# Neighbourhood attention on one Trainium2 core: transposing the probabilities by a product with diag(1/sum), and a quarter of the evictions on VectorE

## The chip, the cores and the metric

One core of one Trainium2 chip runs the whole program; all data is fp32. The metric is the device time of one execution in microseconds. Of the core's engines three do the work of the stage at hand: TensorE (matrix products and transposes into PSUM), VectorE and ScalarE (everything elementwise, and the moves out of PSUM, called evictions here).

## The reference, cut to what matters

The model is a block with four mixers and experts, followed by two layers of a second block. Each of these two layers has a neighbourhood attention: 512 tokens stand on a grid of 8 rows by 64 columns, with 8 heads of width 64. A query attends in one softmax to its window of the grid (all 8 rows, 16 columns, with a bias per offset) and to 256 context keys.

```
s_win = einsum("bhqd,ibhqjd->bhqij", q_r, k_win) * scale + bias
s_ctx = einsum("bhqd,bkhd->bhqk", q_r, k_ctx) * scale
p = softmax(concatenate([s_win, s_ctx], axis=-1), axis=-1)
o = einsum("bhqij,ibhqjd->bhqd", p_win, v_win) + einsum("bhqk,bkhd->bhqd", p_ctx, v_ctx)
```

## The kernel before, in words

A tile of 128 queries takes, in the order in which the kernel holds the tokens, the keys of its own 128 tokens and of 64 on either side. `neighbourhood_attention` (line 3143) runs once per layer. It makes queries, keys and values first, and then builds a list of *quads*: one quad is a pair of heads and two query tiles, so a layer has 4 pairs x 2 = 8 quads. A quad has two *steps*, one per query tile t (0 to 3), each with two *entries*, one per head. A layer has 16 steps; four of them in a row make a pair of heads. An entry has n local keys (192 for t of 0 and 3, 256 for t of 1 and 2) and 256 context keys, so its row of scores is 448 or 512 wide.

`attend` (line 411) turns the quads into groups. For step i:

- *score* (lines 427 to 435, TensorE): q against the keys, with 64 contraction rows, into two PSUM banks, one per head. Its eviction is the *mask* (line 440, VectorE): it adds the bias table (or zeros) and writes S in SBUF, with partial maxima, and line 444 reduces them.
- *exp* (line 454, ScalarE): in place in S, with the sum of the row.
- *norm* (lines 469 to 476, VectorE): the reciprocal of the sums, and one `tensor_scalar` per entry that multiplies the whole row of S by it, in place.
- *turn* (lines 478 to 507): per entry one group of up to four transposes of 128 keys (or 64) into one bank, by line 492, or by a product with the identity (line 490) where the output starts at partition 64. That is the case only for t = 3, whose last local chunk has 64 keys at p0 = 64. For t = 0 the first chunk has 64 keys at p0 = 0. ScalarE evicts the bank to PT with one instruction per run of chunks that lie side by side: three for t = 0 and 3, one for t = 1, two for t = 2.
- *weigh* (lines 509 to 524, TensorE, then VectorE's copy): PT against the values, once per quad.

An fp32 product of the source appears in the trace as two records of LDWEIGHTS and MATMUL, a transpose as one. For a transpose, and for the product with the identity, the chunk of S is the loaded operand and the identity the moving one, 128 columns wide.

The order of the work is written out in lines 526 to 546. Iteration i puts score(i+2), norm(i+1), turn(i), exp(i+2), and where a quad has just ended, the weigh of the quad before. `products` (line 237) gives this list to every engine, and each engine runs its own members of it strictly in that order, with semaphores to the others: a group's products wait for what it `needs` and for the eviction of the group that had its bank; an eviction waits for its `after`. S has three slots, so the mask of step i+2 waits for the evictions of step i-1. Scores have two pairs of banks, everything else four single banks. Lines 3256 to 3259 put two remaining value products (vs) between the first iterations. `attend` also serves four other attentions, with the same code.

Of the kernel before, what the change touches and what calls it, by code (L numbers as in the profile page):

```python
# [16 lines left out]
ALU = mybir.AluOpType  # L17
# [3 lines left out]
P = 128  # L21
BANK = 512
# [195 lines left out]
def group(pe, evac, on, tile=None, after=(), needs=(), other=None, pool="", reads=(), dma=False):  # L218
    return Group(pe, evac, on, tile, after, needs, other, pool, reads, dma)
# [188 lines left out]
    return groups  # L408


def attend(M, st, name, quads, heads, nk, chunks, bufs=None, pool="scores"):

    slots = 3
    S, PT = bufs or (st.sb(f"{name}_S", [P, slots, heads, nk]), st.sb(f"{name}_PT", [P, 2, 2, chunks, 2 * P]))
    part_max = st.sb(f"{name}_part_max", [P, 4, heads, 2])
    neg_max = st.sb(f"{name}_neg_max", [P, 4, heads])
    total = st.sb(f"{name}_total", [P, 4, heads])  # L420
    scale = st.sb(f"{name}_scale", [P, 4, heads])
    steps = [(q, x, entries) for q, quad in enumerate(quads) for x, entries in enumerate(quad.steps)]
    N = len(steps)
    masked = steps[0][2][0].masks is not None
    scored, maxed, exped, normed, turned, weighed = {}, {}, {}, {}, {}, {}

    def score(i):
        entries = steps[i][2]

        def pe(pe_, bank):  # L430
            for j in range(len(entries[0].parts)):
                for e, entry in enumerate(entries):
                    c0, q, k, n = entry.parts[j]
                    last = pe_.matmul(bank[:, e * BANK + c0:e * BANK + c0 + n], q, k, start=True, stop=True)
            return last

        def mask(dve, bank, link):
            for e, entry in enumerate(entries):
                for j, (c0, n, m) in enumerate(entry.masks):
                    link.post(dve.tensor_tensor_reduce(  # L440
                        S[:, i % slots, e, c0:c0 + n], bank[:, e * BANK + c0:e * BANK + c0 + n], m, 1.0, -3.0e38,
                        ALU.add, ALU.max, part_max[:, i % 4, e, j:j + 1]))
            dve.wait_ge(link.sem, link.n)
            return dve.tensor_reduce(neg_max[:, i % 4, :], part_max[:, i % 4, :, 0:len(entries[0].masks)], AX,
                                     ALU.max, negate=True)

        def exp_bank(act, bank, link):
            return act.activation(S[:, i % slots, 0, 0:entries[0].n], bank[:, 0:entries[0].n], ACT.Exp,
                                  bias=neg_max[:, i % 4, :], accum_out=total[:, i % 4, :])

        def exp_rows(act, _, link):
            for e, entry in enumerate(entries):
                s = S[:, i % slots, e, 0:entry.n]
                last = act.activation(s, s, ACT.Exp, bias=neg_max[:, i % 4, e:e + 1],
                                      accum_out=total[:, i % 4, e:e + 1])
            return last

        free = turned.get(i - slots, [])
        if masked:
            scored[i] = group(pe, mask, "v", after=free, pool=pool)  # L460
            exped[i] = group(None, exp_rows, "s", after=(scored[i],))
        else:
            scored[i] = exped[i] = group(pe, exp_bank, "s", after=free, pool=pool)
            maxed[i] = group(None, lambda dve, _, link: dve.tensor_reduce(
                neg_max[:, i % 4, :], scored[i].bank[:, 0:entries[0].n], AX, ALU.max, negate=True),
                "v", reads=(scored[i],))
            scored[i].after += (maxed[i],)

    def norm(i):
        def ev(dve, _, link):  # L470
            link(dve.reciprocal(scale[:, i % 4, :], total[:, i % 4, :]))
            for e, entry in enumerate(steps[i][2]):
                s = S[:, i % slots, e, 0:entry.n]
                last = dve.tensor_scalar(s, s, scale[:, i % 4, e:e + 1], None, ALU.mult)
            return last
        normed[i] = group(None, ev, "v", after=(exped[i],))

    def turn(i):
        q, x, entries = steps[i]
        turned[i] = []  # L480
        free = (weighed[q - 2],) if q >= 2 else ()
        for e, entry in enumerate(entries):
            for a in range(0, len(entry.turns), 4):
                some = entry.turns[a:a + 4]

                def pe(pe_, bank, e=e, some=some):
                    for y, (c0, n, p0, _) in enumerate(some):
                        out, keys = bank[p0:p0 + n, y * P:(y + 1) * P], S[:, i % slots, e, c0:c0 + n]
                        if p0:
                            last = pe_.matmul(out, keys, M.ident[:, :], start=True, stop=True)  # L490
                        else:
                            last = pe_.transpose(out, keys, M.ident[:, :])
                    return last

                def ev(eng, bank, link, entry=entry, some=some):
                    y = 0
                    while y < len(some):
                        _, n, p0, chunk = some[y]
                        z = y + 1
                        while z < len(some) and some[z][1:] == (n, p0, chunk + z - y):  # L500
                            z += 1
                        half = entry.half * P
                        last = move(eng, PT[p0:p0 + n, q % 2, entry.head % 2, chunk:chunk + z - y, half:half + P],
                                    bank[p0:p0 + n, y * P:z * P].rearrange("p (c n) -> p c n", n=P))
                        y = z
                    return last
                turned[i].append(group(pe, ev, "s", needs=(normed[i],), after=free))

    def weigh(q):
        quad = quads[q]  # L510
        done = [g for i in range(N) if steps[i][0] == q for g in turned[i]]

        def pe(pe_, bank):
            first, count = set(), {}
            for side, *_ in quad.weigh:
                count[side] = count.get(side, 0) + 1
            for side, v, chunk, p0, n, a, b in quad.weigh:
                count[side] -= 1
                last = pe_.matmul(bank[side * HD:(side + 1) * HD, a:b], v,
                                  PT[p0:p0 + n, q % 2, side, chunk, a:b],  # L520
                                  start=side not in first, stop=count[side] == 0)
                first.add(side)
            return last
        weighed[q] = group(pe, lambda eng, bank, link: quad.out(eng, bank[:, 0:quad.width], link), "v", needs=done)

    order = []
    for i in range(-2, N + 1):
        now = []
        if i + 2 < N:
            score(i + 2)  # L530
            now.append(scored[i + 2])
            if not masked:
                now.append(maxed[i + 2])
        if 0 <= i + 1 < N:
            norm(i + 1)
            now.append(normed[i + 1])
        if 0 <= i < N:
            turn(i)
            now += turned[i]
        if i + 2 < N and masked:  # L540
            now.append(exped[i + 2])
        if i >= 1 and (i == N or steps[i][0] != steps[i - 1][0]):
            weigh(steps[i - 1][0])
            now.append(weighed[steps[i - 1][0]])
        order.append(now)
    return order
# [367 lines left out]
def branches_ab(M, oT_a, oT_b, big, c_in, c_extra):  # L914
# [4 lines left out]
    with Stage(nc, "ab") as st:  # L919
# [62 lines left out]
        with Stage(nc, "b_att") as sb:  # L982
            products(M, "b_att", sum(attend(M, sb, "b", quads, 2, T, TT), []), pools=PAIRED_BANKS)
# [2159 lines left out]
def neighbourhood_attention(M, L, l, hT, yT, sums):  # L3143
# [3 lines left out]
    with Stage(nc, f"na{l}") as st:  # L3147
        qT = st.sb("qT", [P, 4, T])
        kT = st.sb("kT", [P, 4, TA * P])
        v = st.sb("v", [P, TA, NA_W])  # L3150
# [3 lines left out]
        heads = st.sb("heads", [P, 2 * 2 * 5 * 2 * P])  # L3154
        S_rows = st.sb("S", [P, 3, 2, BANK])
# [6 lines left out]
        PT = heads[:, :].rearrange("p (q h c n) -> p q h c n", q=2, h=2, c=5)  # L3162
# [48 lines left out]
        turned = []  # L3211
        for i, (x, xT) in enumerate(((q, qT), (k, kT))):
            turned += transposes(
                M, lambda t, j, x=x: x[:, t, j * P:(j + 1) * P], None, TT, 4,
                evac=lambda eng, bank, link, j, a, n, xT=xT, i=i: scaled(
                    eng, xT[:, j, a * P:(a + n) * P], bank, gains[:, i:i + 1]),
                needs=[(g, gain) for g in made[i, 0] + made[i, 1]])
        gs = context + [gain] + qk[0] + qk[1] + bias[0:1] + qk[2] + bias[1:2] + qk[3] + bias[2:4] + qk[5] + work[0, 0]
        gs += qk[4] + work[1, 0] + qk[6] + work[1, 1] + vs[0:1] + work[0, 1] + vs[1:2] + turned
        quads = []  # L3220
        for pair in range(MH // 2):
            for t0 in range(0, TT, 2):
# [29 lines left out]
                def out(eng, bank, link, pair=pair, t0=t0):  # L3252
                    return move(eng, yT[:, pair, t0 * P:(t0 + 2) * P], bank)
                quads.append(Quad(steps, weigh, out, 2 * P))
        order = attend(M, st, f"na{l}", quads, 2, BANK, 5, (S_rows, PT))
        order[0][0].needs += tuple(context + turned)
        order[0][0].after += tuple(bias)
        order[4][-1].needs += tuple(vs)
# [932 lines left out]
```

How the kernel before makes its waits and increments, by code:

```python
    def __call__(self, ins):  # L137
        self.n += 1
        ins.then_inc(self.sem, 1)
        self.eng.wait_ge(self.sem, self.n)
# [53 lines left out]
    def load(self, sp):  # L194
        while self.issued < len(self.tiles):
            i = self.issued
            if self.slot[i] >= len(self.bufs):
                break
            if self.prior[i] is not None:
                if self.prior[i] not in self.last_group:
                    break
                sp.wait_ge(self.groups_done, self.last_group[self.prior[i]])
            src = self.tiles[i][0]
            sp.dma_start(self.view(i), src(sp) if callable(src) else src).then_inc(self.landed[self.slot[i]], 16)
            self.issued += 1
# [1 line left out]
    def arrived(self, pe, i):  # L207
        pe.wait_ge(self.landed[self.slot[i]], 16 * self.turn[i])
# [58 lines left out]
    def wait_moves(eng, of):  # L267
        for on in "vsg":
            counts = [g.count for g in of if g.on == on and not g.dma]
            if counts:
                eng.wait_ge(moved[on], max(counts))
        for g in of:
            if g.dma:
                eng.wait_ge(g.landed, 16)
# [10 lines left out]
        @block.tensor  # L285
# [5 lines left out]
                    seen = g.tile  # L291
                if g.other is not None:
                    W.arrived(pe, g.other)
                wait_moves(pe, g.needs)
                if g.before:
                    pe.wait_ge(moved[g.before.on], g.before.count)
                g.pe(pe, g.bank).then_inc(W.groups_done, 1)
# [325 lines left out]
    def first_pe(pe, bank):  # L623
        pe.wait_ge(sig["ident"], 1)
        pe.wait_ge(sig["x_in"], 16)
```

## Time and profile before

| | us |
|---|---|
| median of 3 runs (lowest, highest) | 4005.0 (4003.53, 4009.11) |
| the profiled execution, its own time | 4002.32 |
| its span, first to last instruction | 4000.6 |
| TensorE busy | 3719.4 (93%) |
| VectorE busy | 1670.9 (42%) |
| ScalarE busy | 757.1 (19%) |
| GpSimd busy | 175.2 (4%) |
| mean granted clock of TensorE | 0.970 |

Busy times are sums over the whole span, in which many stages follow each other. The time of one stage has to be read from its own window. Neighbourhood attention from its first scores to its last eviction lies from 2322 to 2396 us (layer 0) and from 3313 to 3387 us (layer 1). Ends of matrix products are modelled, so their starts are the firmer numbers. Where the trace says that an engine waited, it names the instruction that came last before it could go on.

### The profile page before, as it was taken

Reading aid. Unit: us, or ns where it says so; the run is one execution under the profiler, and the core shown is the slowest. Engines: PE = TensorE matmul, PEld = TensorE weight load, DVE = VectorE, ACT = ScalarE, POOL = GpSimd, SP = SyncE. Lnnn points to the kernel's source line nnn. Section 1 sums busy time; section 2 is a strip of 40 time slices with the busy share of each in tenths; the row PEclk is TensorE's granted clock in tenths of the full one; section 3 lists DMA queues with packets and bytes.
Section 4 is the critical chain, followed back from the end, with each engine's and each line's share of the span. In section 5 each row is a group of like instructions: output and inputs, shape, how many; then the busy total and the mean of one; then the engine's idle time right before and its main releaser. Section 6 shows DMA issues by size and latency. Waiting matters only on the chain. (4 is left out here: it accounts for less than half of the span.)

```text
span 4000.6 us, 40393 instructions
## 1 busy us (share of the span) xinstructions
PE 3719.4 (93%) x15836; PEld 2158.8 (54%) x15836; DVE 1670.9 (42%) x3004; ACT 757.1 (19%) x1707; POOL 175.2 (4%) x393
## 2 busy tenths in 40 slices
PE   8988899989799899999788999999998999999999
PEld 4654786745334345455345554488444545448844
DVE  0128533546222111111345564554455556355445
ACT  1212201211122010000224352110002435110000
POOL 1001000000000000000203000000000300000000
PEclk9989999998898999999899999999999999999999
DMA  8542012233675888988531022222223111121221
GB/s 316 179 167 96 26 54 96 85 147 121 242 288 201 321 353 334 370 335 357 193 117 62 22 70 93 76 85 85 84 84 114 43 39 47 74 89 69 85 97 51
DMA packets 197969, 576.40 MB, mean 144 GB/s; under 512 B 24580, under 2 KB 34612, under 8 KB 184776
## 3 DMA queue, kind: packets, MB, share of 16 engines
q1 hardware_dynamic: 177008, 515.15, 34.4%
q10 hardware_dynamic: 12888, 32.14, 2.3%
q0 software_dynamic: 7888, 26.53, 1.9%
q8 instruction: 129, 2.11, 0.2%
q14 instruction: 56, 0.46, 0.0%
HBM read 541.80 MB, written 32.00 MB: 143 GB/s over the span
## 5 line engine op out<-in xcount | busy, mean ns | idle before, releaser
L346 PE MATMUL ps<-out_sums 128*128 128x256 f32 (+1 forms) x1152 | 333.6, 450 | 2.3 <-issue 2.3
L346 PEld LDWEIGHTS ps<-out_sums 128*128 128x128 f32 x1152 | 218.7, 190 | 114.2 <-issue 94.5
L346 PE MATMUL ps<-ring,mixers_xT 128*128 128x256 f32 (+2 forms) x1024 | 254.0, 402 | 14.0 <-DMA ring<-in_w_in 7.1
L346 PEld LDWEIGHTS ps<-ring,mixers_xT 128*128 128x128 f32 x1024 | 195.7, 201 | 61.4 <-issue 22.2
L346 PE MATMUL ps<-mixers_xT,ring 128*128 128x512 f32 (+1 forms) x480 | 209.2, 594 | 2.6 <-DMA ring<-in_w_in 1.7
L346 PE MATMUL ps<-ring,layers_hT 128*128 128x512 f32 x416 | 187.0, 607 | 19.8 <-PEq L276 18.9
L346 PE MATMUL ps<-ring,ctx_hT 128*128 128x512 f32 (+2 forms) x448 | 166.7, 531 | 27.5 <-PEq L127 16.7
L2306 PE MATMUL ps<-ring,mixers_xT 128*64 128x512 f32 x400 | 177.1, 599 | 7.5 <-issue 6.5
L2307 PE MATMUL ps<-ring,mixers_xT 128*64 128x512 f32 x400 | 176.9, 599 | 0.0
L346 PE MATMUL ps<-ring,out_hidden 128*128 128x512 f32 x384 | 167.4, 592 | 0.0
L346 PEld LDWEIGHTS ps<-mixers_xT,ring 128*128 128x128 f32 (+1 forms) x480 | 88.6, 187 | 117.5 <-issue 113.6
L346 PEld LDWEIGHTS ps<-ring,layers_hT 128*128 128x128 f32 x416 | 79.8, 195 | 120.4 <-issue 118.1
L346 PEld LDWEIGHTS ps<-ring,ctx_hT 128*128 128x128 f32 x448 | 82.3, 196 | 107.5 <-issue 105.5
L346 PE MATMUL ps<-out_hidden 128*128 128x512 f32 x288 | 127.4, 599 | 6.2 <-issue 6.2
L2347 DVE TENSOR_TENSOR moe_h<-moe_sg,ps 128x512 f32<-128x512 f32 x17 | 11.7, 689 | 271.5 <-PE ps L2307 259.2
L2306 PE MATMUL ps<-ring,moe_hT 128*64 128x512 f32 x224 | 104.0, 619 | 21.4 <-DMA ring<-in_e_down 11.3
L346 PEld LDWEIGHTS ps<-ring,out_hidden 128*128 128x128 f32 x384 | 73.0, 190 | 91.0 <-issue 90.9
L346 PE MATMUL ps<-layers_hT,ring 128*128 128x256 f32 x512 | 115.3, 387 | 5.1 <-ACT out_rms_rs L2641 5.1
L2306 PEld LDWEIGHTS ps<-ring,mixers_xT 128*64 128x64 f32 x400 | 54.0, 138 | 121.9 <-issue 121.9
L346 PE MATMUL ps<-ring,layers_yT 128*128 128x512 f32 x256 | 112.8, 592 | 0.0
L346 PEld LDWEIGHTS ps<-layers_hT,ring 128*128 128x128 f32 x512 | 99.5, 195 | 19.6 <-issue 5.5
L346 PE MATMUL ps<-ring,ctx_ins 128*128 128x512 f32 x232 | 102.9, 602 | 6.9 <-ACT ctx_ins L3282 3.3
(855 smaller groups left out, 6057.0 us busy)
## 6 DMA issues: line engine op xcount, KB each, us to landing
ring<-in_w_ff SPq DMA_DIRECT2D x45, 2048.0 KB, 13.0
ring<-in_w_in SPq DMA_DIRECT2D x43, 2048.0 KB, 10.6
ring<-in_e_down SPq DMA_DIRECT2D x28, 2048.0 KB, 8.8
ring<-in_e_gate SPq DMA_DIRECT2D x26, 2048.0 KB, 15.9
ring<-in_e_up SPq DMA_DIRECT2D x26, 2048.0 KB, 12.6
ring<-in_w_ada SPq DMA_DIRECT2D x24, 2048.0 KB, 11.6
deep_ring_more<-in_e_up SPq DMA_DIRECT2D x7, 2048.0 KB, 9.9
deep_ring_more<-in_e_gate SPq DMA_DIRECT2D x7, 2048.0 KB, 15.5
```

The lines of the kernel that those rows point to most:

```text
L346: last = pe.matmul(out, lhsT, rhs, start=(j == 0), stop=(j == len(pairs) - 1))
L2306: pe.matmul(bank[0:HALF, :], left(k)[:, 0:HALF], wa[:, k, cols], **ends)
L2307: last = pe.matmul(bank[HALF:P, :], left(k)[:, HALF:P], wb[:, k, cols], **ends)
L2347: lambda eng, bank, link, i=i: eng.tensor_tensor(h[:, i, :], sg[:, i, :], bank, ALU.mult),
```

## The change

`attend` gets an argument `diagonal`, which only the neighbourhood attention sets. With it, norm no longer touches S: it multiplies the identity (128 x 128) by the reciprocal sums of an entry and writes a diagonal matrix `diag`, in three slots. Every transpose of a chunk of S becomes a product of that chunk with the diagonal matrix, which transposes and scales in one. And of the two evictions in steps with an odd number, the second (e = 1) is given to VectorE instead of ScalarE: 1 of 4 groups. The other attentions keep their code.

```diff
-def attend(M, st, name, quads, heads, nk, chunks, bufs=None, pool="scores"):
+def attend(M, st, name, quads, heads, nk, chunks, bufs=None, pool="scores", diagonal=False):
...
+    diag = st.sb(f"{name}_diag", [P, slots, heads, P]) if diagonal else None
...
                 s = S[:, i % slots, e, 0:entry.n]
-                last = dve.tensor_scalar(s, s, scale[:, i % 4, e:e + 1], None, ALU.mult)
+                out, s = (diag[:, i % slots, e, :], M.ident[:, :]) if diagonal else (s, s)
+                last = dve.tensor_scalar(out, s, scale[:, i % 4, e:e + 1], None, ALU.mult)
...
-                        if p0:
+                        if diagonal:
+                            last = pe_.matmul(out, keys, diag[:, i % slots, e, :], start=True, stop=True)
+                        elif p0:
                             last = pe_.matmul(out, keys, M.ident[:, :], start=True, stop=True)
                         else:
                             last = pe_.transpose(out, keys, M.ident[:, :])
...
-                turned[i].append(group(pe, ev, "s", needs=(normed[i],), after=free))
+                turned[i].append(group(pe, ev, "v" if diagonal and i % 2 and e else "s", needs=(normed[i],), after=free))
...
-        order = attend(M, st, f"na{l}", quads, 2, BANK, 5, (S_rows, PT))
+        order = attend(M, st, f"na{l}", quads, 2, BANK, 5, (S_rows, PT), diagonal=True)
```

## Rows read from the trace of the kernel before

**Rows 1.** Windows of the two attention stretches: us, busy and (instructions) of each engine, clock.
```profile
2322.00:2396.00 74.00, 66.83 (x459) 40.65 (x457) 44.15 (x203) 45.82 (x139) 0.00 (x0) 1.00 0.09 30
3312.90:3386.80 73.90, 67.67 (x459) 41.14 (x460) 44.71 (x202) 45.09 (x138) 0.00 (x0) 1.00 0.09 30
```

**Rows 2.** Timeline of TensorE: start, us, instruction, count, [idle before <-releaser].
```profile
2344.53 1.09 PE L492 MATMUL ps<-ident,na_S 128*128 128x128 f32 x8 [0.75 <-DVE na_S L474]
...
2355.36 0.38 PE L434 MATMUL ps<-na_kT,na_qT 64*128 64x256 f32 x2
2355.67 1.09 PE L492 MATMUL ps<-ident,na_S 128*128 128x128 f32 x8
2356.70 1.03 PE L434 MATMUL ps<-na_kT,na_qT 64*128 64x192 f32 x8
2358.47 1.09 PE L492 MATMUL ps<-ident,na_S 128*128 128x128 f32 x8 [0.75 <-DVE na_S L474]
```

**Rows 3.** Lines by form, layer 1's stretch: xcount | busy us, mean ns | idle before.
```profile
L492 PE MATMUL ps<-ident,na_S 128*128 128x128 f32 x112 | 17.7, 283 | 4.1 <-DVE na_S L474 4.1
L492 PE MATMUL ps<-ident,na_S 128*64 128x128 f32 x8 | 2.3, 285 | 0.0
L490 PE MATMUL ps<-ident,na_S 128*64 128x128 f32 x16 | 3.5, 298 | 0.0
L474 DVE TENSOR_SCALAR na_S<-na_S,na_na_scale 128x512 f32<-128x512 f32 x16 | 7.1, 484 | 0.3
L474 DVE TENSOR_SCALAR na_S<-na_S,na_na_scale 128x448 f32<-128x448 f32 x16 | 6.5, 451 | 0.3
```

**Rows 4.** Lines view of layer 0's stretch, the transposes.
```profile
L492 PE MATMUL ps<-ident,na_S 128*128 128x128 f32 (+1 forms) x120 | 18.2, 283 | 4.3 <-DVE na_S L474 4.3
```

**Rows 5.** Waits of TensorE in the 75 us behind layer 0's stretch: total, times, longest.
```profile
PE ps L346 <- PEq L276: 0.9, 1, 0.9
```

**Rows 6.** Timeline of TensorE where other shapes stand beside the transposes.
```profile
2332.91 1.06 PE L492 MATMUL ps<-ident,na_S 128*64 128x128 f32 x8
2333.81 7.03 PE L346 MATMUL ps<-ring,layers_hT 128*128 128x512 f32 x16
2340.77 0.43 PE L434 MATMUL ps<-na_kT,na_qT 64*128 64x192 f32 x2
```

**Rows 7.** Source view of line 1302: ns min/median/max, first and last start.
```profile
L1302 PE MATMUL ps<-c_first_pair,cd_work x16: 251/251/272, 443.1 to 444.8; 128*128 128x2 f32 x16
```

**Rows 8.** Timeline of TensorE, a step of the last query tile.
```profile
2377.03 0.33 PE L492 MATMUL ps<-ident,na_S 128*128 128x128 f32 x1
2377.28 0.43 PE L490 MATMUL ps<-ident,na_S 128*64 128x128 f32 x2
2377.65 0.55 PE L492 MATMUL ps<-ident,na_S 128*128 128x128 f32 x3
```

**Rows 9.** Source view of line 474: the scaling in another stage, four widths.
```profile
L474 DVE TENSOR_SCALAR b_att_b_S<-b_att_b_S,b_att_b_scale x16: 281/385/491, 377.7 to 394.6; 128x128 f32<-128x128 f32 x4, 128x256 f32<-128x256 f32 x4, 128x384 f32<-128x384 f32 x4, 128x512 f32<-128x512 f32 x4
```

**Rows 10.** Source view of line 340: VectorE's copies out of PSUM, 512 and 256 wide.
```profile
L340 DVE COPY mixers_xT<-ps x46: 680/683/692, 10.4 to 1870.4; 128x512 f32<-128x512 f32 x46
L340 DVE COPY layers_yT<-ps x32: 424/425/425, 2176.5 to 3384.9; 128x256 f32<-128x256 f32 x32
```

**Rows 11.** Timeline of VectorE: first mask and the scaling of one step.
```profile
2355.90 0.36 DVE L440 CUSTOM_DVE_ANT_0 na_S<-ps,na_table 128x192 f32<-128x192 f32 x1 [0.64 <-PE ps L434]
...
2357.53 0.88 DVE L474 TENSOR_SCALAR na_S<-na_S,na_na_scale 128x512 f32<-128x512 f32 x2
```

**Rows 12.** Timeline of TensorE at the end of layer 0's stretch.
```profile
2383.90 1.09 PE L492 MATMUL ps<-ident,na_S 128*128 128x128 f32 x8
2386.70 1.09 PE L492 MATMUL ps<-ident,na_S 128*128 128x128 f32 x8 [1.70 <-DVE na_S L474]
...
2392.92 2.10 PE L519 MATMUL ps<-na_heads,na_v 128*64 128x256 f32 x20 [1.11 <-ACT na_heads L338]
```

**Rows 13.** Timeline of ScalarE there: the last step's evictions.
```profile
2391.06 1.80 ACT L338 ACTIVATE na_heads<-ps 128x128 f32<-128x128 f32 x6 [2.40 <-PE ps L492]
```

## The prediction

> **What bounds the kernel now.** I read the windows by stage first, because the page's shares are means over stages that have nothing to do with each other, and the change touches only the two attention stretches that line 3255 makes, one per layer: 74 us each from the first score to the last eviction [rows 1]. TensorE is busy in them for 66.8 and 67.7 us, VectorE for 44 to 45, ScalarE for 45 to 46, at a granted clock of 1.00, so the clock has nothing to give or lose. TensorE works in the order of the list, so I then read its timeline. Of the four steps of a pair of quads, one per query tile, step 2 begins its transposes at 2344.53, and in the next pair at 2358.47: 13.9 us, with one hole, where VectorE's scaling is late [rows 2]. Its idle is 0.75; the last score record starts 0.31 before a block that comes unhindered (2355.36, 2355.67) and ends 0.38 after its start, so 0.07 more is lost: 0.82. The lines view puts all that TensorE idles before transposes, waiting for the scaling, at 4.1 us in layer 1 and 4.3 in layer 0 [rows 3, 4]; 1.70 of each is in the last pair [rows 12], the rest is three waits a layer, one in each of the other pairs. With 0.07 for each: 2.6 and 2.8, 5.4 us in both. So the stage is TensorE's, with small holes that VectorE makes. The next stage is TensorE's too: its one wait in 75 us is 0.9 us [rows 5], so it hides no delay.
>
> **What is removed and added on TensorE.** A step is one query tile with two heads. Each head has four transposes, so 32 steps have 256, of which 16 are products with the identity already (line 490, p0 is 64): the lines view of a layer gives 112 + 8 transposes and 16 records of line 490, two for each of 8 products [rows 3]. So 240 transposes become fp32 products with two records each, as line 490's have.
>
> One transpose: eight take 1.09 us, the last of them 0.27, so seven intervals in 0.82, of which the first is 0.16, as in line 490's pair [rows 8], and the others 0.109 [rows 2]. One product: no row has full 128x128 weights with 128 moving columns and no transpose, so I bound it. From below by the moving columns: 16 records of 512 columns in 7.03 us, less 0.59 for the last, over 15, is 0.429, so 0.107 for 128, 0.214 for two [rows 6]. By the weights: 16 records with full weights and only 2 moving columns start from 443.1 to 444.8, 1.7 over 15 intervals, 0.11 each, which can only be the loads [rows 7]; two give 0.22. From above: line 490's pair takes 0.43 less 0.27, 0.16 for one interval [rows 8], 0.32 for two records. I take 0.222, twice 0.111, since 0.16 also stands between the first two transposes after any change of tile shape, where nothing is loaded ahead, and 0.109 behind it. So +0.113 for each of 240: **+27.1 us**. The bounds are +0.105 (25.2) and +0.21 (50).
>
> Change of shape: a group that uses another part of the array than the one before starts late. From line 346's 128x128 to line 434's 64x128 the start is 2340.77 where 2333.81 + 7.03 - 0.59 + 0.43 = 2340.68 was due: 0.09; from transposes to line 346, 2332.91 + 1.06 - 0.27 + 0.11 = 2333.81, nothing [rows 6]. So it is the shape that costs, not the passing from transpose to product, and with the 0.05 of the first interval a change costs 0.15. In the last step of four, transpose to 64-column product starts 0.25 after and back 0.37 after the pair's start: 0.11 + 0.14 and 0.21 + 0.16 [rows 8]. These changes stay. New ones come where t is 0: its first transpose of each head has 64 columns and today costs no change (eight in 1.06 [rows 6]); as a product of 64 columns it has line 490's shape. The block then goes through the shapes 64, 128, 64, 128 where it was of one: three more changes, 0.44, in 8 steps: **+3.5 us**, bound from below by 0. The Trainium skill bears on this (TensorEngine Tiling (Array Packing), Key Properties): changing the tiling mode drains the engine; its Restrictions say that column tiling rules out the transpose mode for fp32, so the 64-column transposes would be untiled today. By that rule the 3.5 us stand and without it they go; the trace agrees, in the 0.09 and in the missing gap.
>
> The skill also has a rule against the change: transpose mode is "4× faster for FP32" (TensorE: Matmul & The Clock Gate, Terms). The trace shows a factor of 2, since 128 columns of an fp32 product take 0.214; the price by the page is rival 4.
>
> **What is removed on VectorE.** The scaling of 448 or 512 elements (mean 451, 484 ns [rows 3]) becomes two products of a 128x128 identity with the sum's reciprocal: 281 ns, the shortest form in another stage [rows 9]. Two scalings of 512 take 0.88 [rows 11]; two of 128 take 0.88 - 2 x 0.20 = 0.47. So the chain from a score to the next transposes loses 0.40. It runs today: last score record from 2355.36, masks from 2355.90, with the reduction and the reciprocal to 2357.53, scaling to 2358.41, transposes at 2358.47: 3.1 us from that last score record's start [rows 2, 11]; after, 2.7. TensorE's own way from that record, in an odd step, is 0.31 to the transposes, 1.03 for them (2355.67 to 2356.70) and 0.65 + 0.31 for a score: 2.30 today, 0.8 less than the chain, which is the wait; with +0.90 for eight products 3.20 after, 0.5 more than the chain. After an even step the weighing (2.1 [rows 12]) lies there as well. So the six waits go: **-5.4 us**.
>
> In the last pair there is no score between steps 13 and 14, and the idle is larger: transposes at 2383.90, end of their issue 0.93 later, next at 2386.70: 1.87 [rows 12]. After: the chain is 0.40 shorter and TensorE 0.90 later, 0.57 left. **-1.3 us** a layer, 2.6 in all.
>
> **What VectorE gets.** In odd steps the second head's eviction goes to it, 16 of 64. Step 1 has one copy of 128x512 (0.69), step 3 three (128, 128 and 256 wide), about 0.86 by 0.69 for 512 and 0.42 for 256 with 0.07 of overlap each [rows 10]. They stand in its queue behind the next step's scaling and ahead of the next mask. What they could delay is that mask: the products' end is 0.27 after their last record, the copy ends at 1.03 (step 3: 1.2), and the mask cannot start before 0.20 + 0.65 + 0.54 = 1.39 after it, as the score comes behind the products (0.54 is 2355.36 to 2355.90 [rows 2, 11], 0.65 is the score's 1.03 less its last record's 0.38, 0.20 is 0.11 and 0.09 for the change of shape). It is covered by 0.2 to 0.36 us; without that cover it would be 0.86 x 16 = 14 us at most, as rival 3. ScalarE, with up to 1.80 of evictions a step [rows 13], only gets lighter. The final weighing waits for ScalarE's six pieces (2391.06 + 1.80, start 2392.92 [rows 12, 13]); with three on VectorE beside them I give 0.1 a layer, **-0.2 us**. The weighing's one more semaphore costs nothing that rows show.
>
> **Sum.** 27.1 + 3.5 - 5.4 - 2.6 - 0.2 = **+22.4 us**. The profiled execution took 4002.3 us with a span of 4000.6; it becomes 4024.7. The three runs have a median of 4005.0, 2.7 above it, so I forecast **4027 us**, 0.56% slower. No change that a measurement can tell is within 0.2%, 8 us.
>
> **Rivals.** 1. A second record that waits for its weights at every product (0.16 + 0.11): +0.05 x 240 = 12 more, **4039**. For it: the only pairs of line 490 do this. Against: 0.11 with full weights in sixteen successive records [rows 7]. Chance 0.10.
> 2. The 0.15 at a block's edges belongs to transposes after all: two edges in 24 steps (7 us), six in 8 steps (7 us), and 3.5 that doesn't come: 17 less, **4010**. Against it: no gap between transposes and line 346 [rows 6]. Between this and the forecast lies that only the 64-column part is wrong, 4023. Chance 0.06 for 4010.
> 3. VectorE's copies stop the next mask: a third of 14 us, **4032**. For it: cover is only 0.2 us. Against: everything ahead on TensorE got longer. Chance 0.07.
> 4. A product costs four transposes: 3 x 0.109 x 240 = 78.5 in the place of 27.1, **4078**. Against: 0.107 for 128 columns [rows 6]. This is what the skill's rule would make. Chance 0.02.
> 5. The other side: TensorE isn't the bound. Its ends are modelled; were the period set by the hand-offs (score, mask, scaling, transposes), the passes would fit in and only the 8.2 us of waits would go: **3997**. It decides if a product costs under 8.2/240 = 0.034 more than a transpose. For it: VectorE's 0.40 is real and on the chain three times a layer. Against: in four steps TensorE issues without a hole but for one. Chance 0.06.
>
> The forecast has 0.69, with its own range of 4021 to 4033. The range, 4013 to 4039, takes in rivals 1 and 3 and most of the way to 2, and leaves about 0.15 outside. Faster: half of rival 5 and a little, 0.04; within 0.2%: the other half and half of rival 2, 0.07; slower 0.89.
>
> **What the changed profile would show.** The product line with 512 records in both layers, 0.111 from one record to the next, and blocks of 16 in 1.72 + 0.27 where eight took 1.09; blocks of t = 0 longer by about 0.44 than those of t = 1 or 2. No idle on TensorE for VectorE's scaling but one of 0.6 a layer. A pair of quads 13.9 - 0.8 + 3.4 + 0.44 = 17.0 us long, and each stretch of 74 us 11 us longer. VectorE: 64 products of 128x128 at about 0.28 and its masks still starting 0.53 after the last score record. I am wrong if the interval of records is not 0.11, if waits of 0.5 us and more stay in the middle of the stretch, or if the next stage, after 0.9 us of waits, starts as early as before.

## The result and the profile after

| | before | after |
|---|---|---|
| median of 4 runs, us | 4005.7 (4003.5 to 4009.1) | 4031.8 (4029.3 to 4034.3) |
| ratio, 95% interval | | 1.0070 (1.0057 to 1.0083) |
| profiled execution, its own time (span) | 4002.3 (4000.6) | 4034.3 (4032.6) |
| TensorE, VectorE, ScalarE busy | 3719, 1671, 757 | 3754, 1673, 749 |

The kernel is 26.0 us slower by the medians; the forecast was 22.4, and 4031.8 lies in the range. The profiled execution is the slowest of the four after, and 32 us above that of before, so the first thing to read is how much of it lies in the changed stretches. Windows of the two stretches (us, busy and instructions of TensorE, weight loads, VectorE, ScalarE, GpSimd, then the clock), which answer to [rows 1]:

```profile
2328.60:2415.40 86.80, 83.49 (x579) 56.54 (x578) 45.08 (x219) 41.66 (x123) 0.00 (x0) 1.00 0.07 25
3329.50:3416.30 86.80, 83.49 (x579) 56.52 (x578) 45.08 (x219) 41.68 (x124) 0.00 (x0) 1.00 0.08 25
```

They are 86.8 us long where they were 74.0 and 73.9. From a layer's first score to the next block's first product it is 85.7 in both layers (2329.56 to 2415.28 in layer 0), where it was 73.0 and 72.8: 12.7 and 12.9 us, **25.6 us** together. The other 6.4 us lie in stages that are the same in both programs. The window from the start to the first score, before and then after:

```profile
0.00:2322.90 2322.90, 2107.53 (x9988) 1211.90 (x9988) 793.65 (x1622) 439.64 (x984) 133.16 (x284) 0.96 0.52 195
```

```profile
0.00:2329.50 2329.50, 2109.69 (x9988) 1212.68 (x9988) 794.37 (x1622) 439.70 (x984) 132.53 (x284) 0.96 0.52 194
```

The same 9988 matrix records, the same engines' work, 6.6 us more. Programs that are alike up to there scatter as much: in the profile of run 2 below the first score starts at 2319.7 us, in that of run 7 at 2328.0. The medians, which even some of this out, differ by 26.0. So from here on I compare the lengths of the stretches, which are the same within 0.3 us from layer to layer of one kernel (but for runs 6 and 8, where the clock differs), and take the run times only as a check.

The timeline of TensorE after, the four steps of a pair, answers to [rows 2, 8]:

```profile
2367.12 2.05 PE L492 MATMUL ps<-na_na_diag,na_S 128*128 128x128 f32 x16
2369.10 1.03 PE L435 MATMUL ps<-na_kT,na_qT 64*128 64x192 f32 x8
2370.06 2.05 PE L492 MATMUL ps<-na_na_diag,na_S 128*128 128x128 f32 x16
...
2375.28 2.72 PE L492 MATMUL ps<-na_na_diag,na_S 128*128 128x128 f32 x16
2377.93 1.14 PE L435 MATMUL ps<-na_kT,na_qT 64*128 64x256 f32 x8
2379.00 2.52 PE L492 MATMUL ps<-na_na_diag,na_S 128*64 128x128 f32 x16
```

A block of sixteen records takes 2.05 us for query tiles 1 and 2, where eight transposes took 1.09; 2.72 for tile 3, where it was 1.90; and 2.52 for tile 0, where it was 1.06. After the score each of them starts without a wait. By form, layer 1's stretch, the records of line 492 and the short scaling, which answer to [rows 3]:

```profile
L492 PE MATMUL ps<-na_na_diag,na_S 128*128 128x128 f32 x224 | 32.4, 288 | 0.3 <-DVE na_na_diag L476 0.3
L492 PE MATMUL ps<-na_na_diag,na_S 128*64 128x128 f32 x32 | 6.9, 298 | 0.0
L476 DVE TENSOR_SCALAR na_na_diag<-ident,na_na_scale 128x128 f32<-128x128 f32 x32 | 7.7, 284 | 0.6
```

There are 256 records a layer and 0.3 us of waits for the scaling, where there were 4.1 and 4.3 in the two layers. The scaling takes 284 ns (281 was forecast). The end of layer 0's stretch, against [rows 12]:

```profile
2401.76 2.05 PE L492 MATMUL ps<-na_na_diag,na_S 128*128 128x128 f32 x16
2404.16 2.05 PE L492 MATMUL ps<-na_na_diag,na_S 128*128 128x128 f32 x16 [0.34 <-DVE na_na_diag L476]
...
2412.24 2.10 PE L523 MATMUL ps<-na_heads,na_v 128*64 128x256 f32 x20 [1.20 <-DVE na_heads L340]
2415.28 1.10 PE L346 MATMUL ps<-ring,layers_hT 128*128 128x512 f32 x2 [0.94 <-PEq L276]
```

The only wait for the scaling that is left is between steps 13 and 14, and the last weighing now waits for VectorE's eviction (1.20) and not ScalarE's (1.11).

### The profile page after: what moved, and what is told of

It reads as the page before. It is cut to its first block and busy times, and to the rows that moved or that the text cites. A ratio compares the mean times of both kernels' runs of the same rounds, so it can differ in the third digit from the quotient of the medians.

```text
span 4032.6 us, 40873 instructions
## 1 busy us (share of the span) xinstructions
PE 3754.5 (93%) x16076; PEld 2190.7 (54%) x16076; DVE 1673.4 (41%) x3036; ACT 748.9 (19%) x1675; POOL 174.7 (4%) x393
```

## The experiments

Each kernel is one or two edits away from the kernel before, the changed one, or the experiment named. In runs made from the kernel before, `diagonal=True` only marks the calls of the neighbourhood attention and writes no diagonal matrix. The length of a stretch (layer 0, layer 1) is again from the layer's first score to the next block's first product, in the profile of that kernel.

| kernel | stretches, us | run time, us | ratio to before, 95% interval |
|---|---|---|---|
| before | 73.0, 72.8 | 4001.5 to 4005.7 (medians of four sets) | |
| after | 85.7, 85.7 | 4031.8 | 1.0057 to 1.0083 |
| 1 diagonal only | 85.6, 85.6 | 4027.2 | 1.0042 to 1.0075 |
| 2 evictions only | 72.7, 72.7 | 4002.7 | 0.9992 to 1.0012 |
| 3 products with the identity | 86.2, 86.1 | 4028.0 | 1.0047 to 1.0080 |
| 4 short scaling only (leaves out the scaling by the sums) | 71.4, 71.3 | 4001.2 | 0.9990 to 1.0009 |
| 5 after, full width | 81.2, 81.2 | 4020.6 | 1.0029 to 1.0060 |
| 6 before, full width | 74.2, 72.5 | 4001.5 | 0.9991 to 1.0010 |
| 7 scaling ahead of mask | 69.7, 69.4 | 3998.6 | 0.9980 to 0.9998 |
| 8 = 6 and 7 | 70.2, 68.7 | 3997.7 | 0.9981 to 0.9998 |
| 9 = 8, merged evictions | 67.6, 67.6 | 3993.2 | 0.9964 to 0.9984 |
| 10 = 9, one eviction on VectorE | 66.1, 66.1 | 3989.0 | 0.9947 to 0.9975 |

### 1. The diagonal without the moved evictions

```diff
-turned[i].append(group(pe, ev, "v" if diagonal and i % 2 and e else "s", ...
+turned[i].append(group(pe, ev, "s", ...
```

> The changed kernel with every eviction back on ScalarE. The changed kernel's two attention stretches are 12.7 and 12.8 us longer than before (25.5 in all; the rest of its 28 to 32 us lies in stages that are the same in both). Theory 1, all of the loss is the products' second record and the changes of shape on TensorE, and who evicts is without effect: the stretches are 12.6 to 12.8 us longer, the last weighing waits 1.3 after the last record where the changed kernel waits 1.47, and the time is 4031 us within 2. Theory 2, the copies on VectorE cost something (its mask of step 2 of a pair then starts later): the stretches come out 1 us or more shorter than the changed kernel's. Theory 3, ScalarE needed the relief: 1 us or more longer.

The last weighing, TensorE's timeline:

```profile
2409.62 2.10 PE L523 MATMUL ps<-na_heads,na_v 128*64 128x256 f32 x20 [1.10 <-ACT na_heads L338]
```

The stretch is 0.1 us shorter, all of it here: the weighing waits 1.10 where the changed kernel waits 1.20. Theory 1. Who evicts had next to no part in the loss: 0.1 us a layer.

### 2. The moved evictions without the diagonal

The line that run 1 took back, put into the kernel before.

> The kernel before with only the quarter of evictions moved to VectorE; transposes and scaling as before. Theory 1: the copy stands behind the next scaling in VectorE's queue and pushes the mask behind it 0.7 us back, but the scaling that comes after that mask still ends 0.5 us or more before TensorE wants it, so the three waits of a layer stay at 0.75 (the two longer ones, 1.09 and 0.94, where ScalarE was late, may fall to it): 4005 us, stretches within 0.7 us of 74. Theory 2: VectorE is on the path in every step, and 8 copies of 0.69 and 8 of 1.04 us come on top: up to 14 us longer, 4019.

Lines view of layer 0's stretch, against [rows 4]:

```profile
L492 PE MATMUL ps<-ident,na_S 128*128 128x128 f32 (+1 forms) x120 | 18.2, 283 | 3.9 <-DVE na_S L474 3.9
```

Idle before transposes falls from 4.3 to 3.9: the third wait is 0.75 like the others now, where it was 1.09, since ScalarE is less late before it: the mask of that step stands 0.34 us for ScalarE's exp, where it stood 0.99. The masks behind the copies start later, as expected (in step 2 of the last pair 1.96 us behind the start of the score, for 1.29), and it costs nothing. Theory 1: the 14 us of theory 2 do not come.

### 3. Products with the identity, nothing else

```diff
-                        if p0:
+                        if p0 or diagonal:
                             last = pe_.matmul(out, keys, M.ident[:, :], start=True, stop=True)
```

> The kernel before with every transpose written as a product with the identity; VectorE still scales the whole rows and ScalarE evicts all. Theory 1: blocks of 1.98, 1.98, 2.65 and 2.46 us for the four steps of a pair, as in the changed kernel, 33.6 us more in all; the six waits of 0.8 go because TensorE itself is 0.96 later, with no help from VectorE; of the wait between steps 13 and 14 0.9 of 1.87 stays (0.4 to 0.6 in the changed kernel). Stretches 13.0 us longer each, time about 4032. Theory 2: it was VectorE's shorter scaling that took the waits away: they stay in part, 0.4 each, and the time is 4034 or more.

TensorE's timeline at steps 13 and 14:

```profile
2401.55 2.05 PE L490 MATMUL ps<-ident,na_S 128*128 128x128 f32 x16
2404.34 2.05 PE L490 MATMUL ps<-ident,na_S 128*128 128x128 f32 x16 [0.74 <-DVE na_S L474]
```

13.2 us a stretch, where 13.0 was expected. The blocks have the changed kernel's lengths, and the three waits of 0.8 a layer are gone with VectorE's long scaling in place. This is the run that settles the matter: products in the place of transposes, with their second record and their changes of shape, are the whole loss, and the waits went because TensorE itself came later. Of the waits that the timeline lists only this last one is longer than in the changed kernel, 0.74 to 0.34.

### 4. The short scaling alone

The changed kernel with two edits: every eviction on ScalarE, and `turn` as before (transposes of S). `diag` is written and not read, so the scaling by the sums is left out of the computation.

> The kernel before, but VectorE writes the diagonal matrices as in the changed kernel and nothing reads them: the scaling by the sums is left out of the computation, and TensorE does the same transposes as before. It prices VectorE's relief alone. Theory 1: the chain from a score to the next transposes is 0.40 us shorter, the six waits fall from 0.82 to 0.42 and the two of the last pair by 0.4: 3.2 us less, 4002.5. Theory 2: the waits have another cause (ScalarE's exp, a bank) and stay: 4005.7, stretches of 74 as before.

A wait in the middle, and the one between steps 13 and 14:

```profile
2347.00 1.09 PE L494 MATMUL ps<-ident,na_S 128*128 128x128 f32 x8 [0.35 <-DVE na_na_diag L476]
...
2387.98 1.09 PE L494 MATMUL ps<-ident,na_S 128*128 128x128 f32 x8 [1.30 <-DVE na_na_diag L476]
```

0.35 where it was 0.75 [rows 2], 1.30 where it was 1.70 [rows 12]: 0.40 each, 1.6 us in either layer, 3.2 in both, as by theory 1. The run time shows nothing of it (ratio 1.0000, within 0.001 or 4 us either way), which is the limit of what run times can tell here. So VectorE's relief is worth 3.2 us with transposes. With products it is worth 0.6 us in layer 0 and 0.5 in layer 1, by runs 3 and 1, which differ in it alone (86.2 and 86.1 against 85.6).

### 5. The changed kernel without narrow products

```diff
                     for y, (c0, n, p0, _) in enumerate(some):
+                        if diagonal and n < P:
+                            c0, n, p0 = c0 - p0, P, 0
                         out, keys = bank[p0:p0 + n, y * P:(y + 1) * P], S[:, i % slots, e, c0:c0 + n]
```

> The changed kernel with no 64-column product: for t = 0 the first chunk's product takes 128 columns of S (the upper 64 rows of its output aren't evicted), for t = 3 it begins 64 columns earlier and fills all partitions (the lower 64 aren't evicted). Same number of products. Theory 1, a change of the array's shape costs TensorE: every block of 16 records becomes alike, 1.78 us from first to last record, where it is 2.25 for t = 0 and 2.45 for t = 3; 0.47 + 0.67 = 1.14 a pair, 9.1 us in eight pairs, nothing of it eaten by a wait, since VectorE's chain (2.7) is well below TensorE's own way (3.2); stretches of 81.1 us, time 9 us below the changed kernel, 0.44% above before. Theory 2, the 0.47 and 0.67 come from narrow loads or the partition offset and not from the change: blocks shrink by less than half of that, as the wider load takes it back.

Tiles 2, 3 and 0:

```profile
2353.09 2.05 PE L494 MATMUL ps<-na_na_diag,na_S 128*128 128x128 f32 x16
...
2356.14 2.05 PE L494 MATMUL ps<-na_na_diag,na_S 128*128 128x128 f32 x16
...
2361.11 2.05 PE L494 MATMUL ps<-na_na_diag,na_S 128*128 128x128 f32 x16
```

All blocks are 2.05 us, with the same count of records and wider loads. 4.6 us less a stretch, 9.1 in all, theory 1 to the tenth. The edit takes out the narrow products together with the changes of shape, so it can't part the two by itself; the starts of single records in the changed kernel can. In tile 3's block it is the full-width product behind a 64-column one that is late: its first record starts 0.20 us after the one before, and its second 0.21 after that, where run 5 has 0.11 and 0.11. So the changes of shape made the blocks of tiles 3 and 0 long, and not slow narrow products alone.

### 6. The same in the kernel before

> The same edit in the kernel before: its 64-column products with the identity (t = 3) become 128-column transposes, and nothing else changes. Blocks of t = 3 fall from 1.63 to 0.82 us from first to last record, 0.81 a pair, 6.5 in all, by theory 1 of the last run. Theory 1 for the time: VectorE's chain of 3.1 to 3.25 us from a score to the next transposes was just hidden behind that block, so a fourth wait of about 0.8 us appears in each pair, before the transposes of t = 0, and the stretches stay within 1 us of 73: 4001 to 4003. Theory 2: TensorE alone counts, the stretches are 3.2 us shorter each and the time 6.5 us lower.

TensorE's timeline: tile 3, score, tile 0:

```profile
2346.02 1.09 PE L494 MATMUL ps<-ident,na_S 128*128 128x128 f32 x8
2347.04 1.14 PE L434 MATMUL ps<-na_kT,na_qT 64*128 64x256 f32 x8
2348.89 1.09 PE L494 MATMUL ps<-ident,na_S 128*128 128x128 f32 x8 [0.71 <-DVE na_S L474]
```

The block of tile 3 takes 1.09 where it took 1.90, and the transposes of tile 0 behind the next score wait 0.71, where they didn't wait. 0.8 us a pair is gained and about as much lost to VectorE's chain: the stretch of layer 1 is 0.4 shorter. Theory 1. In layer 0 it is 1.2 longer, for another reason (run 8).

### 7. The scaling ahead of the mask, in odd iterations

```diff
         now = []
+        if 0 <= i + 1 < N and diagonal and i % 2:
+            norm(i + 1)
+            now.append(normed[i + 1])
         if i + 2 < N:
             score(i + 2)
```

(and not once more behind it). `diagonal` only marks this call here.

> The kernel before, but in odd iterations the scaling of step i+1 stands ahead of the mask of step i+2 in the list (in even ones it stays behind). Nothing is added or taken away. Its exp is done by 2355.69, the mask starts at 2355.90 today and would start at about 2356.9, with its own exp and scaling still 0.8 us ahead of TensorE. Theory 1, the waits are VectorE's order alone: the three waits of 0.82 to 1.16 in each layer vanish and the one between steps 13 and 14 falls from 1.87 to 0.3: stretches of 68.7 us, 8.6 us less in all, 0.2% faster. Theory 2: exp isn't ready, VectorE stands before the scaling and the mask comes 2 us late: the waits move to the blocks of t = 3 and the time is the same or longer.

VectorE's queue: the scaling of step 2, then the mask of step 3, which stood the other way round in [rows 11]:

```profile
2346.50 0.15 DVE L471 RECIPROCAL na_na_scale<-na_na_total 128x2 f32<-128x2 f32 x1
2346.69 0.88 DVE L474 TENSOR_SCALAR na_S<-na_S,na_na_scale 128x512 f32<-128x512 f32 x2
2347.49 0.35 DVE L440 CUSTOM_DVE_ANT_0 na_S<-ps,na_table 128x192 f32<-128x192 f32 x1
```

and TensorE's last two waits for a scaling, steps 14 and 15:

```profile
2387.65 1.09 PE L492 MATMUL ps<-ident,na_S 128*128 128x128 f32 x8 [0.43 <-DVE na_S L474]
...
2391.58 0.33 PE L492 MATMUL ps<-ident,na_S 128*128 128x128 f32 x1 [0.66 <-DVE na_S L474]
```

No wait is left in the middle of the stretch. It is 3.3 and 3.5 us less in the two layers, where 4.3 was expected: the order does remove the waits (theory 1), but a new one of 0.66 stands before step 15, whose mask and exp now come later; that place I hadn't looked at.

### 8. Both edits

> Both edits of the last two runs in the kernel before: 128-column transposes everywhere and the scaling ahead of the mask in odd iterations. Theory 1: with the waits gone by the order, the 0.81 us a pair of the narrow products comes through: 8.6 + 6.5 = 15 us less, stretches of 65.5 us, time 0.38% below before. Theory 2: ScalarE, with 11.3 us of evictions and exp in a pair that would last 12.3 us, is late by then and takes a part: stretches of 67 to 69 us, 8 to 12 us less.

This is the edit of run 6 and that of run 7 together, in the kernel before. 67 to 69 was expected by theory 2, and it is 68.7 in layer 1: ScalarE is late now. Its timeline, then VectorE's:

```profile
2352.57 1.27 ACT L338 ACTIVATE na_heads<-ps 64x128 f32<-64x128 f32 x6
2353.73 0.73 ACT L454 ACTIVATE na_S<-na_S,na_na_neg_max 128x512 f32<-128x512 f32 x1
```

```profile
2352.69 0.16 DVE L444 TENSOR_REDUCE na_na_neg_max<-na_na_part_max 128x2 f32<-128x4 f32 x1
...
2355.29 0.17 DVE L471 RECIPROCAL na_na_scale<-na_na_total 128x2 f32<-128x2 f32 x1 [0.95 <-ACT na_S L454]
```

VectorE has the mask of step 2 done at 2352.85; ScalarE is still evicting step 0 and begins the exp at 2353.73, so VectorE stands 0.95 us for it. In the middle of the stretch TensorE waits for this only once, 0.41 us. The loss is at the end: before step 14 the same thing happens with step 12's evictions, and TensorE waits 1.49, where it was 0.43 in run 7. ScalarE, VectorE and TensorE there:

```profile
2378.85 1.27 ACT L338 ACTIVATE na_heads<-ps 64x128 f32<-64x128 f32 x6
```

```profile
2381.56 0.17 DVE L471 RECIPROCAL na_na_scale<-na_na_total 128x2 f32<-128x2 f32 x1 [1.17 <-ACT na_S L454]
```

```profile
2382.70 1.09 PE L494 MATMUL ps<-ident,na_S 128*128 128x128 f32 x8 [1.49 <-DVE na_S L474]
```

In layer 0 another 1.5 us are lost, by the windows before, in and behind the last weighing:

```profile
2380.00:2389.00 9.00, 5.46 (x44) 3.73 (x44) 4.15 (x18) 6.57 (x21) 0.00 (x0) 1.00 0.01 2
2389.20:2392.90 3.70, 3.62 (x20) 1.91 (x20) 0.00 (x0) 0.00 (x0) 0.00 (x0) 0.57 0.00 0
2393.00:2403.00 10.00, 9.20 (x22) 4.21 (x23) 9.55 (x7) 1.20 (x2) 0.00 (x0) 1.00 0.53 136
```

The granted clock is 0.57 in the last weighing, the lower level of 1.2 GHz for most of it, and its twenty records take 3.62 us for 2.10. TensorE had waited three times just before, 1.49, 0.66 and 1.52 us. Run 6 has the same in layer 0 (clock 0.54 in its last weighing, behind waits of 1.71 and 1.52). No other kernel has it here. Layer 1 of run 8, with the same waits, does not have it, in the last weighing too:

```profile
3376.20:3379.30 3.10, 2.10 (x20) 1.28 (x21) 0.57 (x2) 0.01 (x1) 0.00 (x0) 1.00 0.00 0
```

So the waits alone do not explain it, and what decides is left open.

### 9. Chunks of 64 keys evicted over all partitions, merged

The order of run 7, and this in the place of run 6's edit:

```diff
-                        turns = [(0, P if t else HD, 0, t - t0),
-                                 (P if t else HD, HD if kind == 2 else P, HD if kind == 2 else 0, t - t0 + 1)]
+                        turns = [(0, P, 0, t - t0), (P if 0 < t < TT - 1 else HD, P, 0, t - t0 + 1)]
```

> The last kernel (128-column transposes everywhere, scaling ahead of the mask in odd iterations), whose 64-key chunks are now evicted over all 128 partitions too, so that the local chunks of a head leave in one instruction: four evictions a step for t = 0 and 3 where there were six. The other half of those chunks isn't read. In the last kernel the stretches were 70.2 and 68.7 us where TensorE's records allow 65.5, and ScalarE was what was late. Theory 1, ScalarE is the next bound: it loses 0.6 us for t = 3, 0.1 for t = 0, the last weighing comes 0.5 earlier, the wait between steps 13 and 14 (1.66) falls by 0.5: 1 to 2 us less per layer, stretches of 67 to 68.5, time 0.15 to 0.25% below before. Theory 2, the order on VectorE bounds it (exp waits for a mask that comes late): unchanged but for the last weighing, 0.5 less per layer.

The wait between steps 13 and 14:

```profile
2380.73 1.09 PE L492 MATMUL ps<-ident,na_S 128*128 128x128 f32 x8 [1.39 <-DVE na_S L474]
```

This wait is 1.39 where it was 1.49, and the last weighing waits 0.80 where it waited 1.52; the rest of the 1.1 us gained in layer 1 lies in small waits before. Layer 0 gains 2.6 us, since the clock stays at its upper level. Theory 1, with less of it in this wait than expected.

### 10. One eviction in eight on VectorE

Run 9 and this line:

```diff
-turned[i].append(group(pe, ev, "s", needs=(normed[i],), after=free))
+turned[i].append(group(pe, ev, "v" if diagonal and i % 4 == 0 and e else "s", needs=(normed[i],), after=free))
```

> The same, and the second head's eviction of t = 0 goes to VectorE, which stood 0.95 us before the scaling of step 2 waiting for ScalarE's exp. Theory 1: ScalarE's exp of step 2 comes 0.6 earlier, VectorE's copies fill its own wait: stretches of 66.5 to 68, 0 to 1 us less per layer than the run before. Theory 2: the copy stands in VectorE's queue until TensorE has turned the step and then holds up what is behind it, 0.7 us for each of four pairs: stretches 1 us or more longer than in the run before.

Windows of both stretches, then TensorE's waits in layer 0's:

```profile
2327.20:2394.40 67.20, 63.64 (x451) 40.16 (x450) 46.73 (x211) 40.61 (x107) 0.00 (x0) 1.00 0.09 33
3308.00:3375.10 67.10, 63.55 (x450) 40.11 (x450) 46.62 (x211) 40.62 (x107) 0.00 (x0) 1.00 0.10 33
```

```profile
PE ps L492 <- DVE na_S L474: 1.0, 2, 0.7
PE ps L519 <- ACT na_heads L338: 0.8, 1, 0.8
```

66.1 us a stretch, 1.5 less than run 9 and a little better than expected: the eviction fills VectorE's own wait and ScalarE's exp comes earlier, so that the wait before step 14 falls from 1.39 to 0.34. This kernel leaves nothing of the computation out and is **0.39% faster** than the kernel before (ratio 0.9961, 0.9947 to 0.9975), with transposes and the full scaling. Against the changed kernel it is 19.6 us less a stretch.

## Why the prediction was right, step by step

- **TensorE is the bound of the stretch, VectorE only makes holes.** Right (runs 3 and 4). Rival 5, that the hand-offs are the bound, is out: then run 3 would have cost nothing, and it cost 13.2 us a stretch.
- **240 products of two records at 0.111.** The interval is 0.112: sixteen records of 2.05 - 0.27 = 1.78 us have 15 intervals, of which the first is 0.21 (below), the others 1.57/14. The bound taken from [rows 7], 0.11, was the price. That the loads set it, as the prediction says, is not shown: the bound by the moving columns, 0.107, lies close, and no run parts the two. Rival 1 (0.16 at each second record) and rival 4 (four times a transpose) are out.
- **Changes of shape.** Right in kind (run 5), too small in size: this is the term that was off. I took 0.15 for a change, 0.05 of it for the first interval behind it, by line 490's 64-column pair and by the first two transposes. With full-width fp32 products the interval after a change is longer. First two records of a block, after and then before:

```profile
2370.06 0.49 PE L492 MATMUL ps<-na_na_diag,na_S 128*128 128x128 f32 x2
```

```profile
2369.61 0.44 PE L492 MATMUL ps<-ident,na_S 128*128 128x128 f32 x2
```

Less the length of the last record, 0.275 and 0.272, and before rounding, that is 0.213 for products and 0.165 for transposes. So blocks of tiles 1 and 2 grew by 0.96 (0.90 forecast), of tile 3 by 0.82 (0.68), of tile 0 by 1.46 (1.34): 4.2 us a pair, 33.6 in all, for 30.6 (27.1 + 3.5). The three new changes in tile 0's block are near the forecast, 2.52 - 2.05 = 0.47 for 0.44; run 5 takes them out. Rival 2, that the price is the transposes' own, is out: products have it too, and more of it. The Trainium skill (TensorEngine Tiling (Array Packing), Key Properties) states that a change of the tiling mode drains the engine. The 9.1 us of run 5 agree with that; no run shows the drain itself.
- **Six waits go, -5.4; in the last pair -2.6.** Right: the six went and the last pair's shrank, 33.6 - 25.6 = 8.0 us for 8.2 in the sum (5.4, 2.6, and 0.2 for the last weighing). What is left between steps 13 and 14 is 0.34 in the listed wait, and by the starts, as the prediction reckoned it, 2404.16 - 2401.76 - 1.78 - 0.11 = 0.51, for 0.57. The text gave VectorE's 0.40 a share in the six; run 3 shows that they would have gone without it.
- **VectorE's copies are covered.** Right, with less to spare than I gave, and rival 3 is out. Three copies take 1.04, not 0.86; step 3's end just before the next mask, VectorE's timeline:

```profile
2395.43 1.04 DVE L340 COPY na_heads<-ps 128x128 f32<-128x128 f32 x3 [0.35 <-PE ps L492]
2396.58 0.42 DVE L441 CUSTOM_DVE_ANT_0 na_S<-ps,na_table 128x256 f32<-128x256 f32 x1
```

The mask starts 0.57 after the last score record and not 0.54, so this cover is used up (the copy ends at 2396.47); run 1 shows that it cost nothing.
- **The last weighing, -0.2.** Wrong in sign, +0.2: with three pieces on VectorE it waits 1.20 and without them 1.10 (run 1), a layer. The three copies of 1.04 us, reckoned at 0.86, are what it waits for.
- **The median.** Forecast 4027, measured 4031.8: 3.2 of the 4.8 us are the stretches (25.6 for 22.4); the rest lies in stages that the change does not touch, which scatter by more than that. The 3.2 are 3.0 from the blocks and 0.2 from the waits and the weighing.

## What to carry to other kernels

Folding a scaling into fp32 transposes turned one record into two on TensorE; before giving VectorE's work to TensorE, ask which of them is the bound of that stretch, and count records, not instructions of the source. A hole that another engine leaves on the bound engine can sometimes be closed by the order of that engine's own queue (run 7, 3.4 us a layer), while a cut on the bound engine alone (run 6) only moved the hole. Where TensorE is the bound, try to keep products that follow each other in one shape of the array, even where it means moving columns that nobody reads (run 5, 9.1 us).

## What the runs showed of the hardware that I had not expected

After a change of the array's shape the second record of a full-width fp32 product came 0.21 us after the first, of a transpose or a 64-column product 0.16, and from then on 0.11. And behind waits of 1.49, 0.66 and 1.52 us the granted clock was 0.57 over 3.7 us (run 8, layer 0), which cost as much again as the longest of them; in layer 1, behind the same waits, it stayed at 1.00.
